# Hybrid decoder layer with a mixture of experts: order and cut of the last transfers, and results stored by expert number

## The reference, cut to what matters

```python
h = layer_norm(ALPHA * x + hybrid_token_mixer(x, ...), ln1_g, ln1_b)   # 512 tokens x 1024
# hierarchical_moe(h): top-1 group of 4, then top-2 of its 8 experts
g_prob = softmax(h @ router_group_w + b);  g_top_p, g_idx = top_k(g_prob, 1)
e_top_v, e_top_i = top_k(e_logits_of_that_group, 2)
weights = softmax(e_top_v) * g_top_p
hid = silu(h @ w_gate[e]) * (h @ w_up[e])          # 32 experts, width 256
ffn = sum over the two experts of weight * (hid @ w_down[e])
out = layer_norm(ALPHA * h + ffn, ln2_g, ln2_b)
```

## Time and profile before

| | |
|---|---|
| Median of 3 runs | 432.66 us (432.59 to 433.03) |
| Profiled execution, its own time | 433.34 us |
| its span, first to last instruction | 431.5 us |
| PE busy | 408.7 us (95%) |
| DVE busy | 186.9 us (43%) |
| ACT busy | 114.3 us (26%) |
| POOL busy | 83.5 us (19%) |
| HBM read, written | 134.41 MB, 12.58 MB: 341 GB/s over the span |
| Granted TensorE clock, mean | 0.991 |

### The profile page before, as it was taken

How to read it: one execution, slowest core, us unless ns; L and a number is a source line. 1 busy time by engine, 2 the same in 40 slices (tenths; PEclk the granted TensorE clock), 3 DMA queues, 4 the chain that set the end, 5 groups by cost and what they waited for, 6 DMA issues and landing times.

```text
span 431.5 us, 6632 instructions
## 1 busy us (share of the span) xinstructions
PE 408.7 (95%) x2578; PEld 276.5 (64%) x2578; DVE 186.9 (43%) x368; ACT 114.3 (26%) x185; POOL 83.5 (19%) x113
## 2 busy tenths in 40 slices
PE   7999999999999999999999999999999997888783
PEld 6888877888888888956556555655555564453331
DVE  2479622499957467864312222221222121211077
ACT  3542376973122002310111111111111110103111
POOL 2220000000000001123233323332332331200124
PEclk9999999999999999999999999999999998999998
DMA  8876531221369999999999999999999999999684
GB/s 264 263 196 198 172 95 28 94 97 22 115 214 419 425 420 420 420 362 396 416 414 414 418 409 416 412 414 414 415 418 417 416 418 416 419 420 417 253 342 195
DMA packets 37377, 139.11 MB, mean 322 GB/s; under 512 B 5107, under 2 KB 17427, under 8 KB 25062
## 3 DMA queue, kind: packets, MB, share of 16 engines
q1 hardware_dynamic: 31184, 126.89, 74.3%
q0 software_dynamic: 6144, 11.84, 7.8%
q10 hardware_dynamic: 22, 0.02, 0.1%
HBM read 134.41 MB, written 12.58 MB: 341 GB/s over the span
## 4 chain that ended last, share of the span: by engine, by line
PE 82%; DMA 11%; SPq 4%; DVE 1%; issue 1%; ACT 0%; DVEq 0%; POOLq 0%
PE bank L1104 21%; PE bank L917 12%; PE bank L919 12%; PE bank L918 12%; PE bank L1133 10%; DMA wgu_first<-in_exp_w_up 6%; PE bank L1094 3%; PE bank L1202 2%; PE bank L1124 2%; SPq L509 2%; DMA xg<-h_rows,x_rows 2%; DMA pair_y<-y_pairs 1%; PE bank L1014 1%; PE bank L900 1%; DMA y_pairs<-ys,y_rows 1%; DMA raw<-in_w_in 1%
## 5 line engine op out<-in xcount | busy, mean ns | idle before, releaser
L1104 PE MATMUL bank<-wgu,xTg 128*64 128x256 f32 x736 | 86.2, 388 | 5.8 <-DMA wgu<-in_exp_w_up 4.8
L1104 PEld LDWEIGHTS bank<-wgu,xTg 128*64 128x64 f32 x736 | 52.0, 139 | 32.6 <-DMA wgu<-in_exp_w_up 5.5
L917 PE MATMUL bank<-xT_hi,w_hi 128*128 128x512 f32 x160 | 63.5, 397 | 0.8 <-DVE xT_lo L1244 0.8
L919 PE MATMUL bank<-xT_hi,w_lo 128*128 128x512 f32 x160 | 62.8, 393 | 0.0
L918 PE MATMUL bank<-xT_lo,w_hi 128*128 128x512 f32 x160 | 62.8, 392 | 0.0
L1544 DVE TENSOR_TENSOR hid<-gated,bank 64x256 f32<-64x256 f32 x32 | 13.5, 423 | 106.8 <-ACT gated L843 106.7
L683 POOL DMA_INDIRECT y_pairs<-ys,y_rows x32 | 32.5, 1015 | 135.5 <-PE bank L1094 103.9
L843 ACT ACTIVATE gated<-bank 64x256 f32<-64x256 f32 x32 | 12.1, 377 | 129.1 <-PE bank L1104 129.1
L1133 PE MATMUL bank<-wdn,hidT 128*64 128x512 f32 x192 | 45.3, 593 | 0.0
L1221 DVE TENSOR_TENSOR w_lo<-raw,w_hi 128x2048 fp32r<-128x2048 f32 x12 | 27.5, 2288 | 26.9 <-ACT w_hi L757 26.9
L678 POOL DMA_INDIRECT xg<-h_rows,x_rows x31 | 31.4, 1014 | 24.8 <-issue 8.3
(11 more groups left out here) (252 smaller groups left out, 496.7 us busy)
## 6 DMA issues: line engine op xcount, KB each, us to landing
wgu<-in_exp_w_gate SPq DMA_DIRECT2D x24, 1024.0 KB
wgu<-in_exp_w_up SPq DMA_DIRECT2D x24, 1024.0 KB
wdn<-in_exp_w_down SPq DMA_DIRECT2D x24, 1024.0 KB
raw<-in_w_in SPq DMA_DIRECT2D x9, 1024.0 KB, 6.0
raw<-in_w_out SPq DMA_DIRECT2D x4, 1024.0 KB, 5.1
wdn_extra<-in_exp_w_down SPq DMA_DIRECT2D x4, 1024.0 KB
wgu_spare<-in_exp_w_gate SPq DMA_DIRECT2D x4, 1024.0 KB
wgu_spare<-in_exp_w_up SPq DMA_DIRECT2D x4, 1024.0 KB
```

Source lines behind the costliest of these rows:

```text
L917: pe.matmul(dst, a_hi, b_hi, start=start, stop=False)
L919: return pe.matmul(dst, a_lo, b_hi, start=False, stop=stop)
L1104: mm = pe.matmul(psum[2 + b][BLOCK * which:BLOCK * which + BLOCK, 0:F], xTg[b][:, j, h * BLOCK:(h + 1) * BLOCK], wgu[s][:, which, k, :], s ...
```

## The change

Five edits. The last gate/up load is cut along its contraction into pieces of 4, 2 and 2 of 8 steps, gate and up of each, with a semaphore for each piece, and TensorE starts on a piece when it is there. The residual rows are loaded by tile, with a semaphore each. The result of a pair is stored by expert number: of a token's two experts the one with the lower number goes to the first half of `y_pairs` (`put_by_expert`), and the weights are exchanged alike. SyncE loads the first results of all tiles when every scatter but that of expert 31 is in, then scale and offset of the second norm (no longer ahead of the scatters), then, with the last scatter in, the second results. TensorE adds the first results of all tiles, then the second results of tiles 1 to 3.

```diff
--- before.py
+++ after.py
@@ -46,6 +46,7 @@
 WARM_UP_FIRST = 8
 LOG_TERMS = 9
 PIECES = 4
+LAST_PIECES = ((0, 4), (4, 6), (6, 8))
 
 
 def hybrid_moe_layer(
@@ -141,6 +142,10 @@
         vexp = sb("vexp", [P, TT])
         wsum = sb("wsum", [P, TT])
         weight = sb("weight", [P, TOP_K, TT])
+        by_choice = sb("by_choice", [P, TOP_K, TT])
+        swapped = sb("swapped", [P, TOP_K, TT])
+        kept = sb("kept", [P, TOP_K, TT])
+        y_put = sb("y_put", [P, TOP_K * TT])
         iota_f = sb("iota_f", [P, 140])
         down4, up_slot_e = iota_f[:, 0:N_GROUPS], iota_f[:, 4:4 + N_EXP]
         up_slot = iota_f[:, 36:36 + BLOCK]
@@ -290,6 +295,7 @@
         router_in = sem("router_in")
         gu_in = [sem(f"gu_in{s}") for s in range(RING)]
         dn_in = [sem(f"dn_in{s}") for s in range(RING)]
+        gu_last_in = [sem(f"gu_last_in{n}") for n in range(len(LAST_PIECES))]
         over_gu_in = sem("over_gu_in")
         over_dn_in = sem("over_dn_in")
 
@@ -369,7 +375,7 @@
         pool_chain = sem("pool_chain")
 
         pairs_in = [[sem(f"pairs_in{t}_{k}") for k in range(TOP_K)] for t in range(TT)]
-        h1_in = sem("h1_in")
+        h1_in = [sem(f"h1_in{t}") for t in range(TT)]
         diag_ready = sem("diag_ready")
         z_summed = sem("z_summed")
         var2_ready = sem("var2_ready")
@@ -563,15 +569,24 @@
                 for u in range(RING):
                     refill_gu(head + u + 1, r)
                     refill_dn(head + u, r)
+            def refill_last_gu():
+                e = N_EXP - 1
+                sp_.wait_ge(gu_summed, used_by(e, 0) + 1)
+                for n, (k0, k1) in enumerate(LAST_PIECES):
+                    for which, w in enumerate((exp_w_gate, exp_w_up)):
+                        sp_.dma_start(gu_place(slot_of(e), which)[:, k0 * F:k1 * F], gu_of(w, e)[:, k0 * F:k1 * F]).then_inc(gu_last_in[n], 16)
+
             for q in range(head + turns * RING, N_EXP):
-                if q + 1 < N_EXP:
+                if q + 2 < N_EXP:
                     refill_gu(q + 1, 0)
+                elif q + 2 == N_EXP:
+                    refill_last_gu()
                 refill_dn(q, 0)
 
             last_of_1 = max(q for q in range(N_EXP) if slot_of(q) == 1)
             sp_.wait_ge(gu_summed, last_of_1 + 1)
-            sp_.dma_start(h1[:, :, :].rearrange("p t (a h) -> p t a h", a=2),
-                          h1_rows.rearrange("(t p a) h -> p t a h", p=P, a=2)).then_inc(h1_in, 16)
+            for t in range(TT):
+                sp_.dma_start(h1[:, t, :], h1_rows[2 * t * P:2 * (t + 1) * P, :].rearrange("(p a) h -> p (a h)", a=2)).then_inc(h1_in[t], 16)
 
             def load_over(j):
                 e = sp_.value_load(over_exp_i[0:1, bass.ds(j, 1)], min_val=0, max_val=N_EXP - 1)
@@ -582,16 +597,17 @@
 
             overflow(sp_, load_over)
 
-            sp_.wait_ge(y_scattered[(N_EXP - 4) % ROWS], 16 * ((N_EXP - 4) // ROWS + 1))
-            sp_.dma_start(ln2g[:, :], row(ln2_g).to_broadcast([P, D])).then_inc(ln2_in, 16)
-            sp_.dma_start(ln2b[:, :], row(ln2_b).to_broadcast([P, D])).then_inc(ln2_in, 16)
 
             n = sp_.value_load(n_over[0:1, 0:1], min_val=0, max_val=MAX_OVER)
             sp_.wait_ge(y_scattered[0], 16 * n + mains(0))
-            for b in range(1, ROWS):
-                sp_.wait_ge(y_scattered[b], mains(b))
-            for t in range(TT):
-                for k in range(TOP_K):
+            for k in range(TOP_K):
+                if k == 1:
+                    sp_.dma_start(ln2g[:, :], row(ln2_g).to_broadcast([P, D])).then_inc(ln2_in, 16)
+                    sp_.dma_start(ln2b[:, :], row(ln2_b).to_broadcast([P, D])).then_inc(ln2_in, 16)
+
+                for b in range(1, ROWS):
+                    sp_.wait_ge(y_scattered[b], mains(b) - (16 if k == 0 and b == (N_EXP - 1) % ROWS else 0))
+                for t in range(TT):
                     src = y_pairs[2 * (k * T + t * P):2 * (k * T + (t + 1) * P), :]
                     sp_.dma_start(pair_y[t][k][:, :], src.rearrange("(p a) h -> p (a h)", a=2)).then_inc(pairs_in[t][k], 16)
             for t in range(TT - 1):
@@ -856,7 +872,7 @@
 
                 act.wait_ge(gu_summed, 4 + 3 * RING)
                 act.activation(diag[:, 0, :], ident[:, :], ACT.Copy, scale=ALPHA).then_inc(diag_ready, 1)
-                act.wait_ge(weights_ready, 1)
+                act.wait_ge(weights_ready, TOP_K)
                 for t in range(TT):
                     for k in range(TOP_K):
                         act.activation(diag[:, 1 + TOP_K * t + k, :], ident[:, :], ACT.Copy, scale=weight[:, k, t:t + 1]).then_inc(diag_ready, 1)
@@ -1094,16 +1110,28 @@
                     mm = pe.transpose(psum[b][:, j * P:(j + 1) * P], rows, ident[:, :])
                 mm.then_inc(xg_turned, 1)
 
-            def gate_up(i, s, b, lag, loads):
-                pe.wait_ge(gu_in[s], 32 * loads)
-                pe.wait_ge(xTg_ready, i + 1)
-                wait_free(pe, hid_ready, i, lag)
-                for k in range(KT):
+            def gate_up_part(s, b, ks):
+                for k in ks:
                     h, j = divmod(k, 4)
                     for which in range(2):
                         mm = pe.matmul(psum[2 + b][BLOCK * which:BLOCK * which + BLOCK, 0:F],
                                        xTg[b][:, j, h * BLOCK:(h + 1) * BLOCK], wgu[s][:, which, k, :],
                                        start=k == 0, stop=k == KT - 1)
+                return mm
+
+            def gate_up(i, s, b, lag, loads):
+                pe.wait_ge(gu_in[s], 32 * loads)
+                pe.wait_ge(xTg_ready, i + 1)
+                wait_free(pe, hid_ready, i, lag)
+                gate_up_part(s, b, range(KT)).then_inc(gu_summed, 1)
+
+            def gate_up_last():
+                i = N_EXP - 1
+                pe.wait_ge(xTg_ready, i + 1)
+                pe.wait_ge(hid_ready, i - 1)
+                for n, (k0, k1) in enumerate(LAST_PIECES):
+                    pe.wait_ge(gu_last_in[n], 32)
+                    mm = gate_up_part(slot_of(i), i % 2, range(k0, k1))
                 mm.then_inc(gu_summed, 1)
 
             def gate_up_first(js):
@@ -1156,7 +1184,10 @@
                     sum_rows(6, 0, hot_slot, hot_y).then_inc(table_summed, 1)
                     turn_main_x(1, 0)
                     return
-                gate_up(q + r * RING, slot_of(q), q % 2, 2, loads_of(q, r))
+                if static(r) and q == N_EXP - 1:
+                    gate_up_last()
+                else:
+                    gate_up(q + r * RING, slot_of(q), q % 2, 2, loads_of(q, r))
                 if q == 1:
 
                     turn_hid(0, 0, 2)
@@ -1188,15 +1219,15 @@
 
             n = pe.value_load(n_over[0:1, 0:1], min_val=0, max_val=MAX_OVER)
             pe.wait_ge(y_copied, n + N_EXP)
-            pe.wait_ge(h1_in, 16)
             pe.wait_ge(diag_ready, 1)
             for t in range(TT):
+                pe.wait_ge(h1_in[t], 16)
                 for h in range(2):
                     pe.matmul(psum[2 * t + h][:, :], diag[:, 0, :], in_order(h1[:, t, :])[:, h * H // 8:(h + 1) * H // 8], start=True, stop=False)
             pe.wait_ge(diag_ready, 1 + TOP_K * TT)
-            for t in range(TT):
-                last = 0 if t < DVE_ADDED else TOP_K - 1
-                for k in range(last + 1):
+            for k in range(TOP_K):
+                for t in range(DVE_ADDED if k else 0, TT):
+                    last = 0 if t < DVE_ADDED else TOP_K - 1
                     pe.wait_ge(pairs_in[t][k], 16)
                     for h in range(2):
                         mm = pe.matmul(psum[2 * t + h][:, :], diag[:, 1 + TOP_K * t + k, :], pair_y[t][k][:, h * H:(h + 1) * H],
@@ -1462,7 +1493,13 @@
             link(v.tensor_tensor(prod[:, :, :, :], counts, chosen[:, :, :, :], ALU.mult))
             link(v.tensor_reduce(rank[:, :], pairs(prod[:, :, :, :]), AX, ALU.add))
             v.tensor_tensor(hot_slot[:, :, :], up_slot.unsqueeze(1).to_broadcast([P, NP, BLOCK]), per_pair(rank[:, :], BLOCK), ALU.is_equal).then_inc(hot_ready, 1)
-            v.tensor_tensor(hot_y[:, :, :], pairs(chosen[:, :, :, :]), per_pair(y_place, N_EXP), ALU.mult).then_inc(hot_ready, 1)
+
+            def put_by_expert():
+
+                link(v.tensor_tensor(swapped[:, 0, :], chosen_e[:, 0, :], chosen_e[:, 1, :], ALU.is_gt))
+                step(v.scalar_tensor_tensor(out=y_put[:, 0:TT], in0=swapped[:, 0, :], scalar=2.0 * T, in1=y_place[:, 0:TT], op0=ALU.mult, op1=ALU.add))
+                link(v.scalar_tensor_tensor(out=y_put[:, TT:], in0=swapped[:, 0, :], scalar=-2.0 * T, in1=y_place[:, TT:], op0=ALU.mult, op1=ALU.add))
+                v.tensor_tensor(hot_y[:, :, :], pairs(chosen[:, :, :, :]), per_pair(y_put[:, :], N_EXP), ALU.mult).then_inc(hot_ready, 1)
 
 
             def copy_xT(i, b, lag):
@@ -1494,6 +1531,7 @@
             v.wait_ge(hid_zero, 2)
             v.wait_ge(xg_turned, 1)
             copy_first_T(1, xTg_ready)
```

(14 more changed lines are left out.)

## The result

| | before | changed |
|---|---|---|
| Median of 4 runs | 432.62 us (432.10 to 433.03) | 437.00 us (436.17 to 437.86) |
| Profiled execution, its own time | 433.34 us | 437.09 us |
| its span | 431.5 us | 435.3 us |

The change makes the kernel slower: the ratio is 1.010 with a 95% interval of 1.0074 to 1.0127, and the forecast was 437.3 us.

The account below looks back on a forecast made before the run. The end was taken as VectorE's start, at the landing of tile 0's second result, plus 16.4 us of its work. First issue -2.75 and queue place +7.4, taken as +4.7 on 432.66, gave 437.3 us; range 434.2 to 439.9.

Parts of the forecast that it names:

- Last gate/up in pieces: Expert 31's gate/up on TensorE: ends 1.95 us earlier; both last scatters issued about 0.85 us earlier.
- First issue: First pair load on SyncE: issued once scatter 30 has landed, at 404.45 for 407.20, 2.75 us earlier.
- no head start: Rival: storing by expert number does nothing at the pair loads; first issue 406.3, sum +6.5, 439.2 us; chance 0.12.
- Place in the queue: Pair loads: second result of tile 0 goes from second to seventh, five places at 1.49 us, 7.4 us later.
- the fit of the Trainium skill: Pair loads: 2.0 us plus bytes at 436 GB/s; seventh landing 10.4 us after issue against 13.0, sum 2.6 us smaller.
- The rule of the Trainium skill against transfers under 1 MiB: Last gate/up pieces: under 75% of peak, last 2.1 MB some 1.1 us later; the prediction did not adopt it.
- VectorE's work: VectorE from its first addition to its last results at the end: 16.4 us, unchanged.
- VectorE has no slack beside it: Kernel before, end stretch: VectorE busy 15.74 of 16.38 us beside TensorE's pair matmuls.
- its stretch shorter than 16 us: Sign that the prediction is wrong: VectorE's final busy stretch under 16 us, meaning it waited for TensorE before.
- The sum: Whole kernel: -2.75 and +7.4 give +4.65, taken as +4.7; span 436.2, own time 438.0, median 437.3 us.
- TensorE as the bound: Rival: TensorE's pair matmuls set the end after the last landing; faster by 1.4 us, 431.3; chance 0.10.
- Loads overlap: Rival: scale and offset cost half, loads run at the weights' pace; queue costs 3.9 to 5.2, 433.9 to 435.1; chance 0.12.

Follow-up runs that it names:

- e3: The kernel before with only the last gate/up load cut into pieces; 433.55 us over 12 runs, ratio 1.0015.
- e5: The changed kernel, but first results also wait for all scatters; 437.36 us, ratio 1.0118 to the kernel before.
- e2: The kernel before with the second result of tile 0 loaded fourth instead of second; 435.49 us, ratio 1.0067.
- e10: As e9, with scale and offset loaded between third and fourth pair load and VectorE waiting for them only at first use; 435.01 us, ratio 1.0056.
- e9: The kernel before with the last gate/up in pieces and the residual rows loaded by tile; 433.01 us over 12 runs, ratio 1.0019.
- e8: The kernel before with last gate/up in pieces, residual rows by tile, and scale and offset right behind the residual rows; 432.22 us over 12 runs, ratio 0.9995.
- e7: The kernel before with only the storing by expert number and the exchanged weights; 432.38 us over 12 runs, ratio 0.9996.
- e12: The kernel before with residual rows by tile, and scale and offset fetched as two rows and spread by TensorE; 435.70 us, ratio 1.0072.
- e11: As e10, with the residual sum of tile 3 computed twice on TensorE; 435.56 us over 12 runs, ratio 1.0059.

## Why the prediction was right, and where its steps were off

By its own steps, in the profiled execution.

*Last gate/up in pieces.* Forecast end 395.05, down of 30 from 396.1, down of 31 from 398.75, scatters at 399.25 and 402.1. Measured 394.64, 395.76, 398.94, 399.11 and 402.30. The price by a small transfer's lower rate did not show. The last scatter starts 0.65 us earlier for the forecast 0.85; that any of it reaches the end by itself is not shown (e3).

*First issue.* Forecast 404.45, measured 404.22. The landing of scatter 30 was right (5.09 us, forecast 5.15). What I took for the alternative was not: I left the last scatter its 4.2 us, and in e5, where the engines are emptier by then, it needs 3.0. By that figure, of the 2.98 us by which the first issue came earlier, 0.65 are the earlier scatter, 1.2 the scatter's shorter landing, and 1.1 the early start itself; the split is an estimate, since the changed kernel's own last scatter shows no landing. The rival "no head start" was priced at +6.5 on this figure; tested, it gave 437.36, 0.4 over the change.

*Place in the queue.* Forecast 12.6 us from first issue to the seventh landing, measured 12.4 (404.22 to 416.65). The mean spacing of the earlier trace rows was the right one to take; the estimate by the fit of the Trainium skill (DMA: Bandwidth & Descriptors, section Anatomy of one DMA), which puts the landing 10.4 us after the issue, came out 2 us short. The rule of the Trainium skill against transfers under 1 MiB (same page, section Bandwidth) did not show in this full queue: the pieces were there before TensorE wanted them, and from 376 to 392 the DMA engines carried 412 GB/s where they had carried 419.

*VectorE's work.* Forecast unchanged at 16.4 us, measured 15.8. This term was mis-sized by 0.6 us, and the sentence "VectorE has no slack beside it" with it. In the kernel before TensorE delivered a tile every 3.44 us (eight matmuls of 0.43) while VectorE needs 3.27 for one (416.74 to 432.56 holds 4.73 for tile 0 and 3.27 for each of tiles 1 and 2). Both were nearly tied, VectorE waiting a little for each tile; the chain's reading was not wrong, only a poor guide to what this change would do. The prediction's own sign for this was "its stretch shorter than 16 us", and it came.

*The sum.* VectorE's start +4.25 (forecast +4.65), its work -0.56, the end behind it +0.1: +3.8 in the span, +3.75 in the execution's own time, against +4.7. The own time was forecast at 438.0 and came out at 437.09. The median came closer (437.0 for 437.3) because the profiled execution of before stood 0.7 us above its median and that of the changed kernel at its median. Part of that closeness is therefore not the forecast's merit.

*Rivals.* TensorE as the bound was ruled out for this change by e2 and by the chain after; but e10 shows the same engine as the bound as soon as tile 0 is served early and tile 1's second result comes sixth. "Loads overlap" did not happen: the landings from the fourth to the seventh are 1.3 us apart, scale and offset no cheaper than the results.

*What stays open.* The pieces and the residual rows by tile, alone or together, never beat the kernel before by the median (433.55, 432.41, 433.01, and 432.22 with the norm's rows moved), though the profiled executions of three of these end 1.4 to 1.9 us before the profiled one of before. The profiled executions lie at the lower end of their kernels' spread (431.41 of 431.41 to 435.01 in e9; 431.57 of 431.17 to 434.20 in e8), and the kernel before has the same spread: 430.88 to 434.30 over 35 runs, its own profiled execution (433.34) in the upper half. So those 1.4 to 1.9 us compare good executions with a poor one. One part the traces show: in e3, e8 and e9 the last scatter starts 1.5 to 1.9 us earlier than in e2 and lands no earlier, at 405.9 to 406.2 for 405.8, with 291 to 321 GB/s in flight at its start for 97. What makes single executions lose 2 to 3 us stays open. The half clock that e2, e3, e7 and e12 show once or twice is a candidate, and the mean granted clocks on record speak for it in e9 (0.989 to 0.994 in the five runs up to 432.18 us, 0.979 to 0.987 in the seven above) and against it as the only cause elsewhere: in e11 as said, and in the kernel before, whose runs at a mean of 0.991 (of those 35) lie anywhere from 430.88 to 433.98 us. No version was found that beats the kernel before.

## What to carry to other kernels

Before the order of loads at the end is changed, ask for each which engine starts on it and how much work that engine has behind it: the engine with the longest work left gets its first input first, and what it needs next right behind (e10). Here moving one 512 KB load from second to fourth place cost 3.0 us, and to seventh place, with the loads begun 3 us earlier, 4.4, though the last load landed no later. An idle stretch of the DMA engines is worth filling only with what is not in front of that input.
